# A paged decode step: who asks for the value pages, SyncE one by one or GpSimd with indirect transfers

## The reference

```
kv_past = cache_kv[page_table, l]            # 8 sequences x 16 pages of 128 rows
q, k, v, logf, gates = project_in(h, ...)    # 16 heads: 4 stick-breaking, 6 dilated, 6 forgetting
o_sb  = stick_breaking_attention(q_sb, k_sb_all, v_sb_all, q_pos, k_pos)
o_fox = forgetting_attention(q_fox, k_fox_all, v_fox_all, cum[:, p:], cum, q_pos, k_pos)
o_dil = merge_dilation_groups(...)           # three window buffers per sequence
x = x + gate1 * (merged @ w_o);  x = x + gate2 * hier_moe(...)
```

## Time and profile before

| | |
|---|---|
| median of 3 runs | 1397.74 us (1393.3 to 1398.04) |
| the profiled execution, its own time | 1395.3 us |
| its span, first to last instruction | 1393.6 us |
| PE busy | 1175.0 us (84%) |
| DVE busy | 436.0 us (31%) |
| ACT busy | 293.7 us (21%) |
| POOL busy | 232.2 us (17%) |
| moved by DMA | 306.60 MB, mean 220 GB/s |
| mean granted clock | 0.921 |

### The profile page before, as it was taken

How to read it: one execution, slowest core, us unless ns; L and a number is a source line. 1 busy time by engine, 2 the same in 40 slices (tenths; PEclk the granted TensorE clock), 3 DMA queues, 4 the chain that set the end, 5 groups by cost and what they waited for, 6 DMA issues and landing times.

```text
span 1393.6 us, 21222 instructions
## 1 busy us (share of the span) xinstructions
PE 1175.0 (84%) x7743; PEld 794.1 (57%) x7743; DVE 436.0 (31%) x1072; ACT 293.7 (21%) x629; POOL 232.2 (17%) x321
## 2 busy tenths in 40 slices
PE   5699999987899999986788788878999479989890
PEld 3477777555577777764555555656735345445440
DVE  4200000264332223313344344442634601111116
ACT  2211010143222222222232232222211011111112
POOL 1000000050011112220000000000000046556530
PEclk9899999998889999999998899997999579899895
DMA  8743333139445421049988889995721479999965
GB/s 298 278 176 128 123 122 110 31 121 301 142 192 183 154 92 47 17 148 317 298 290 262 289 287 301 303 334 201 272 95 46 166 293 381 352 410 402 413 227 197
DMA packets 112838, 306.60 MB, mean 220 GB/s; under 512 B 18966, under 2 KB 33071, under 8 KB 103472
## 3 DMA queue, kind: packets, MB, share of 16 engines
q1 hardware_dynamic: 95600, 251.93, 50.8%
q0 software_dynamic: 16576, 49.10, 9.4%
q10 hardware_dynamic: 576, 4.46, 0.9%
HBM read 304.35 MB, written 45.81 MB: 251 GB/s over the span
## 4 chain that ended last, share of the span: by engine, by line
PE 62%; SPq 15%; issue 8%; DVE 8%; DMA 5%; ACT 2%; POOL 0%; POOLq 0%; DVEq 0%; ACTq 0%
PE psum L940 56%; SPq L608 6%; SPq L612 6%; DVE arena L1846 2%; PE psum L1512 1%; SPq L550 1%; PE psum L1250 1%; DMA wring<-in_w_mod 1%; PE psum L1168 1%; DMA arena<-in_cache_kv 1%; DMA xT<-in_cache_kv 1%; DVE wring L1854 1%; PE psum L1537 1%; DVE wring L1846 1%; DMA hT<-gate_tiles 1%
## 5 line engine op out<-in xcount | busy, mean ns | idle before, releaser
L940 PE MATMUL psum<-hT,wring 128*128 128x272 f32 x1216 | 292.6, 399 | 11.4 <-ACT hT L1568 11.4
L940 PEld LDWEIGHTS psum<-hT,wring 128*128 128x128 f32 x1216 | 230.6, 192 | 76.6 <-issue 15.1
L940 PE MATMUL psum<-arena 128*8 128x128 f32 (+6 forms) x1540 | 179.4, 350 | 12.7 <-issue 7.6
L940 PEld LDWEIGHTS psum<-arena 128*8 128x8 f32 (+4 forms) x1540 | 90.6, 113 | 76.5 <-issue 60.4
L940 PE MATMUL psum<-wring,arena 128*8 128x128 f32 (+3 forms) x976 | 108.0, 390 | 7.2 <-DVE wring L1846 3.5
L940 PE MATMUL psum<-hT,arena 128*128 128x272 f32 (+1 forms) x300 | 77.5, 447 | 19.2 <-issue 10.1
L842 POOL TENSOR_SCALAR wring<-wring,arena 128x384 f32<-128x384 f32 (+6 forms) x32 | 45.7, 1427 | 254.5 <-DVE arena L2102 254.5
L1250 PE MATMUL psum<-small,arena 128*128 128x128 f32 x392 | 63.8, 319 | 27.7 <-DMA arena<-in_cache_kv 24.6
L940 PEld LDWEIGHTS psum<-wring,arena 128*8 128x8 f32 (+3 forms) x976 | 49.7, 109 | 58.3 <-issue 52.4
L790 ACT COPY arena<-psum 128x512 f32<-128x512 f32 x80 | 46.6, 585 | 166.6 <-PE psum L1250 113.0
L1250 PEld LDWEIGHTS psum<-small,arena 128*128 128x128 f32 x392 | 52.7, 165 | 38.2 <-issue 34.1
(11 more groups left out here) (243 smaller groups left out, 1361.7 us busy)
## 6 DMA issues: line engine op xcount, KB each, us to landing
arena<-in_cache_kv SPq DMA_DIRECT2D x128, 320.0 KB, 3.5
wring<-in_w_mod SPq DMA_DIRECT2D x10, 2048.0 KB
xT<-in_cache_kv SPq DMA_DIRECT2D x64, 320.0 KB, 3.6
wring<-in_cache_kv SPq DMA_DIRECT2D x64, 320.0 KB, 3.6
wring<-in_w SPq DMA_DIRECT2D x20, 1024.0 KB
out_dil_sample<-in_cache_dil SPq DMA_DIRECT2D x8, 2044.0 KB, 11.0
arena<-in_w SPq DMA_DIRECT2D x27, 512.0 KB
wring<-in_w_in SPq DMA_DIRECT2D x6, 2048.0 KB
```

The source lines that it names most:

```text
L940: return T.matmul(out, lhsT, rhs, start=start, stop=stop, **k)
```

## The change

SP no longer asks for value pages. The page numbers of all 128 pages are loaded once to all partitions (`v_ids`) and DVE computes from them a table of row numbers, `v_at` = 256 * page + 2 * partition + 1, kept in the storage of `rstd`. POOL asks for each value page with one indirect DMA that takes its 128 row numbers from a column of the table. POOL's loop is unrolled: it asks for all 16 pages of sequence 0 first; then, for each b, it waits for `seq_pv` b, loads `vncur`, asks for the first eight pages of sequence b+1, waits for `sp_ready`, does the four additions, and asks for the other eight. SP's wait for `v_used` is gone; ahead of page 9 it waits for `seq_pv`, since the window rows still share a buffer. DVE waits for the page numbers ahead of the stick-breaking scores.

```diff
+            sp.dma_start(v_ids, I["page_table"].rearrange("(o b) n -> o (b n)", o=1).to_broadcast([P, P])
+                         ).then_inc(sem("ld_pt"), 16)
...
-                    if p == half and b0 >= 2:
-
-                        sp.wait_ge(sem("v_used"), i * 2 * PV_STEPS + PV_STEPS * (b0 - 1))
+                    if p == half + 1 and b0 >= 2:
+
+                        sp.wait_ge(sem("seq_pv"), i * 2 + (b0 - 1))
                     if b0 == 0 and p == 4:
                         attention_done()
-                    page(b0, p, 0, kpage[p % 8], f"ld_k{p % 8 // 2}", free)
-                    if p >= half:
-                        values(b0, p - half)
-                    elif b0:
-                        values(b0 - 1, p + half)
+                    page(p, kpage[p % 8], f"ld_k{p % 8 // 2}", free)
                     if p == half + 1:
                         window_rows()
-                if b0 == NB - 1:
-                    for p in range(half, PAGES):
-                        values(b0, p)
...
+            def settle(scrap):
+
+                link(nc.gpsimd.tensor_tensor(scrap, ones[0:1, 0:1], ones[0:1, 0:1], ALU.mult))
+
+            def values(b, lo, hi):
+
+                for p in range(lo, hi):
+                    pool.indirect_dma_start(
+                        out=vpast[b % 2][:, p, :], out_offset=None,
+                        in_=I["cache_kv"].rearrange("n l k a h d -> (n l k a) (h d)"),
+                        in_offset=bass.IndirectOffsetOnAxis(ap=v_at[:, PAGES * b + p:PAGES * b + p + 1], axis=0)
+                        ).then_inc(sem(f"ld_v{b % 2}"), 16)
+
+            for n in range(2):
+                pool.wait_ge(sem(f"st_g{n}"), 16 * 3)
...
+            pool.wait_ge(sem("v_rows"), 1)
+            settle(pool_scrap)
+            values(0, 0, PAGES)
+            for b in range(NB):
+                if b:
+                    pool.wait_ge(sem("seq_pv"), b)
+                pool.dma_start(vncur[0:NT, :], vs_d[b * NT:b * NT + NT, :]).then_inc(sem("ld_vn"), 16)
+                if b + 1 < NB:
+                    settle(pool_scrap)
+                    values(b + 1, 0, PAGES // 2)
+                pool.wait_ge(sem("sp_ready"), b + 1)
+                sp_, w, y = s_sp, s_w[:, b % 2, :], s_y
...
+                nc.gpsimd.tensor_tensor(y[:, 0:256], w[:, 0:256], w[:, 128:384], ALU.add
+                                        ).then_inc(sem("y_ready"), 1)
+                if b + 1 < NB:
+                    values(b + 1, PAGES // 2, PAGES)
...
+            dve.wait_ge(sem("ld_pt"), 48)
+            ts(v_at, v_ids, 256.0, value_row, ALU.mult, ALU.add).then_inc(sem("v_rows"), 1)
```

More of the change, by code:

```diff
@@ L611, in page @@
                         sp.wait_ge(sem("kT_mm"), free)
-                    sp.dma_start(dst, pg[:, :, kv].rearrange("o k h d -> k (o h d)")).then_inc(sem(done), 16)
-                def values(q0, p):
-                    page(q0, p, 1, vpast[q0 % 2][:, p, :], f"ld_v{q0 % 2}")
+                    sp.dma_start(dst, pg[:, :, 0].rearrange("o k h d -> k (o h d)")).then_inc(sem(done), 16)
                 def window_rows():
@@ L849, in _ @@
             link(nc.gpsimd.memset(s_y[:, 256:320], 0.0))
[L850 to L856, removed]
-                    sp_, w, y = s_sp, s_w[:, par, :], s_y
-                    link(nc.gpsimd.tensor_tensor(w[:, 0:256], sp_[:, 0:256], sp_[:, 16:272], ALU.add))
-                    link(nc.gpsimd.tensor_tensor(y[:, 0:256], w[:, 0:256], w[:, 32:288], ALU.add))
-                    link(nc.gpsimd.tensor_tensor(w[:, 0:256], y[:, 0:256], y[:, 64:320], ALU.add))
-                    nc.gpsimd.tensor_tensor(y[:, 0:256], w[:, 0:256], w[:, 128:384], ALU.add
-                                            ).then_inc(sem("y_ready"), 1)
-                link.leave(NB // 2)
+            def settle(scrap):
+                link(nc.gpsimd.tensor_tensor(scrap, ones[0:1, 0:1], ones[0:1, 0:1], ALU.mult))
@@ new lines, in _ @@
+            pool.wait_ge(sem("o_ev"), 8)
+            pool.wait_ge(sem("w_used"), 12)
+            pool.wait_ge(*done_at("new_ready"))
+            for stored in ("st_k", "st_v"):
+                pool.wait_ge(sem(stored), 16 * KV_STORES)
+            pool.wait_ge(sem("st_smp"), 16 * SAMPLE_STORES)
+            pool.wait_ge(sem("st_lf"), 32)
+            pool.wait_ge(sem("v_rows"), 1)
[10 more added lines that the diff above has]
+                sp_, w, y = s_sp, s_w[:, b % 2, :], s_y
+                link(nc.gpsimd.tensor_tensor(w[:, 0:256], sp_[:, 0:256], sp_[:, 16:272], ALU.add))
+                link(nc.gpsimd.tensor_tensor(y[:, 0:256], w[:, 0:256], w[:, 32:288], ALU.add))
+                link(nc.gpsimd.tensor_tensor(w[:, 0:256], y[:, 0:256], y[:, 64:320], ALU.add))
+                nc.gpsimd.tensor_tensor(y[:, 0:256], w[:, 0:256], w[:, 128:384], ALU.add
+                                        ).then_inc(sem("y_ready"), 1)
+                if b + 1 < NB:
+                    values(b + 1, PAGES // 2, PAGES)
@@ L868, in _ @@
             pool.wait_ge(*done_at("slots_ready"))
-            def settle():
-                link(nc.gpsimd.tensor_tensor(carried[0:1, :], ones[0:1, 0:1], ones[0:1, 0:1], ALU.mult))
             def gather(m):
@@ L877, in gather @@
                     pool.wait_ge(sem("xg_t"), 2 * (m - RING) + 2)
-                    settle()
+                    settle(carried[0:1, :])
                 pool.indirect_dma_start(
@@ L1339, in weigh_values @@
                 if hi < PAGES:
-                    last.then_inc(sem("v_used"), 1)
                     return
```

12 lines of the change are left out of this document (8 added, 4 removed).

## The result

| | before | after |
|---|---|---|
| median | 1395.52 us (4 runs) | 1470.39 us (1465.21 to 1473.95, 4 runs) |
| ratio, 95% interval | | 1.0519 (1.048 to 1.0558) |
| the profiled execution, its own time | 1395.3 us | 1471.75 us |
| its span; mean granted clock | 1393.6 us; 0.921 | 1469.7 us; 0.896 |
| loads of `vncur`, second to eighth | 694.21 to 934.96, 40.1 us each | 709.96 to 1008.20, 49.7 us each |

A forecast was written before the change was run, and what follows sets the result against it. SP's issuing (36.7 us per sequence), PE and the DMA engines were taken to lie close together as bounds. -18.8 (six sequences) - 2 (start) + 0.4 (front) = -20.4 us gave 1377 us, range 1364 to 1402 us.

The forecast's parts named there:

- Six sequences: 6 x (40.1 - 37.0) = 18.8 us less: Decode stage: each of six sequences would shorten from 40.1 to 37.0 us, 18.8 us less in all.
- pitch of 37.0 us: Decode time per sequence: PE's own 36.5 us plus 0.5 us, with an indirect DMA taken as 1.30 us.
- A page lands 3.6 us after its issue ... PE should find its keys there: Decode key pages: SP asks eight pages ahead, over 14 us of PE's work, so PE should not wait for keys.
- DMA engines, 34.4 us per sequence: Decode: 11.7 MB per sequence at 339 GB/s take 34.4 us, only 6% below PE's 36.5 us.
- The rival that made them the bound: Decode: mixed pages reach at most 300 GB/s, 38.9 us per sequence, 1396 us in all, no change; chance 0.17.
- POOL: Decode: indirect DMAs 1.26 us apart, 26 of 36.5 us per sequence, no bound; PE waits 0 to 0.3 us for additions.
- Late additions: Decode rival: eight indirect DMAs at up to 1.77 us delay POOL's additions, PE waits about 3.4 us, 1412 us; chance 0.23.
- PE's own pace, 36.5 us: Decode: PE's time per sequence without waits for pages, the middle of 35.9 and 37.2 us from two sequences.
- The start, 2 us less: First two decode sequences: 2 us less taken, between bounds of 14 us less and 6 us more.
- even sharing: First two decode sequences: POOL's and SP's queues share DMA evenly, so the first sequence ends 6 us later.
- Front, +0.4 us: Before decode: SP's extra page-number load ahead of the 80 small stores costs one issue, 0.4 us more.
- the waits of SP and DVE that I costed at nothing: SP's `seq_pv` wait ahead of page 9 is free; DVE's 2.1 us wait for page numbers hides under PE's 8.75 us.

The follow-up runs named there:

- e12: The changed kernel itself run again, unaltered, on chip 5: 1406.22 us, ratio 1.0064 to the kernel before.
- e18: The changed kernel with only 32 of 128 rows of each value page fetched, on chip 15: 1374.40 us, ratio 0.9846 to the kernel before.
- e11: The changed kernel in its own order, indirect transfers spaced 1.80 us apart, on chip 9: 1402.31 us, ratio 1.0038 to the kernel before.
- e10: The changed kernel with four pages before the additions and twelve behind, transfers 1.47 us apart, on chip 9: 1381.49 us, ratio 0.9887 to the kernel before.
- e5: The changed kernel with plain transfers on POOL's queue and a fifth of each value row, on chip 0: 1372.01 us, ratio 0.9811 to the kernel before.
- e8: The changed kernel with only 32 of 128 rows of each value page fetched, on chip 0: 1371.85 us, ratio 0.9822 to the kernel before.
- e17: The changed kernel with four pages before the additions and twelve behind, transfers 1.47 us apart, on chip 15: 1381.21 us, ratio 0.9901 to the kernel before.
- e9: The changed kernel with four pages before the additions and twelve behind, unspaced, on chip 9: 1386.52 us, ratio 0.9898 to the kernel before.
- e13: The changed kernel with four pages before the additions and twelve behind, unspaced, on chip 5: 1389.89 us, ratio 0.9946 to the kernel before.
- e16: The changed kernel with four pages before the additions and twelve behind, unspaced, on chip 15: 1387.26 us, ratio 0.9963 to the kernel before.
- e15: The changed kernel in its own order, indirect transfers spaced 1.80 us apart, on chip 13: 1407.69 us, ratio 1.0075 to the kernel before.
- e4: The changed kernel with plain transfers on POOL's queue, page number read into a register, on chip 13: 1416.67 us, ratio 1.0143 to the kernel before.
- e1: The changed kernel with value pages asked for two at a time as PE turns key pages, on chip 13: 1411.28 us, ratio 1.0105 to the kernel before.
- e3: The changed kernel fetching 128 of 640 floats of each value row, same bursts, on chip 13: 1471.32 us, ratio 1.053 to the kernel before.

## Why the prediction was wrong, step by step

**"Six sequences: 6 x (40.1 - 37.0) = 18.8 us less"** is the step that failed. Behind its pitch of 37.0 us stand two things that were wrong; this is the first. It put a price on indirect transfers by the time they take POOL, and gave other engines none. On chip 13 they cost (1.0508 - 1.0064), 4.4% or 62 us, in PE's waits for events: the larger part of the loss. No row shown before hinted at it and no rival named it. The trace of the kernel before did carry the chip's mark in its MoE (28 missing records of 288), but PE lost nothing by it there: from 1200 to 1210 us it is busy 10.00 of 10.00 us.

**"A page lands 3.6 us after its issue ... PE should find its keys there"** is the second. That latency was measured with keys and values on one queue, in the order of need; with two full queues it was 9 to 10 us (e12). On chips without the hold-up the forecast was -1.5% (20.4 us) and e12 measured +0.64%, a gap of 29 or 30 us. With a quarter of the rows in each value page, the order alike, e18 stands at -1.5%, 2.2% or 30 us below e12. That this is the forecast's own number is in part luck: e18's pitch of 37.9 us is 0.9 above the forecast's, 5 us in six sequences, and its first two sequences end 6 us earlier than before, at 688.13 us, where 2 were forecast.

**DMA engines, 34.4 us per sequence**: mis-sized. They run at 396 GB/s when both queues are full, so 11.7 MB take 29.5 us, and in e12's sequences they then stand idle for a quarter of the time (share 0.71 to 0.79 where it was 0.92). Bandwidth was less short than I thought, and its order in time mattered more. The rival that made them the bound, 1396 us, is close to e12 by number only.

**POOL**: right. 1.26 us each, and in e12 the additions start 11.05 us after `seq_pv` and end at 14.2; PE waits for them only 2.5 us in the whole stage. The port-pair rule of the Trainium skill that I weighed ("SBUF — State Buffer", the box on the "DVE blocks DMA" trap) doesn't show here: 64 indirect DMAs of the page buffers take 952 to 1077 ns, median 957, with DVE busy a third of each sequence. The rule holds for DVE operations in a two-port mode, and whether any of those beside the transfers ran in one, no run here tells.

**Late additions**, the rival for the slower side: right sign, wrong mechanism. But its price for such a wait was good. e11 fulfils its condition (1.80 us each, 1.77 in the rival), and PE then does wait, for POOL's last addition. The list of PE's waits in e11:

```profile
PE psum L961 <- POOL arena L885: 8.1, 5, 2.0
```

Its pitch is 40.8 us where the rival's sum gave 41.4; e11 is 1.5% above e10.

**PE's own pace, 36.5 us**: 37.7 to 37.9 in e5, e8, e10, e17 and e18, 1.2 us too low for each sequence, 7 us in all. I had taken the middle of two sequences of the kernel before and no loss of clock.

**The start, 2 us less**: measured 15.8 us more (709.96 against 694.21), of it the 15.04 us wait shown above. On chip 5 it was 2.8 us more (697.05), within my bounds of 14 less to 6 more, and near the even sharing that I chose.

**Front, +0.4 us, and the waits of SP and DVE that I costed at nothing**: right, by the rows above.

So with its order mended the idea does what was forecast, nearly: e10 and e17, four pages ahead and twelve behind, 1.47 us apart, are 1.1% and 1.0% faster than the kernel before, and the fastest that leave nothing out. The same order unspaced gave 1.0%, 0.5% and 0.4% (e9, e13, e16). Chip 13 has seen neither.

## What to carry to other kernels

Two queues that are both full don't share by need: what is asked for early on one delays what is needed next on the other, by the bytes of their packets. Where a latency was measured with one queue, bound it again with the second one full before you rely on it. A queue of close indirect transfers may cost engines that have nothing to do with it; space them (e15, 1.0075 on the chip that suffers), or use plain transfers with a page number in a register where a page is contiguous (e4 there: no hold-up, but 1.0143, since bursts of plain transfers delay the keys too). Look in the trace of the old kernel for idle time without a releaser near its own indirect transfers: it marked the chip here. And run the changed kernel itself again beside each experiment: in e5 to e8 I took for the work of my edits what was also a change of chip.

## What was unexpected of the hardware

On one of five numbered chips (13), 128-row indirect DMAs issued 1.26 us apart delay semaphore updates of PE and single instructions of SP's sequencer: a 29 ns MOVE takes up to 707 ns, an event comes up to 14 us late. There the delay outlives the burst a little. Eight transfers started at 710.98 us end on POOL at 720.9, and PE's next transposes start at 723.24:

```profile
723.24 2.39 PE L1269 MATMUL psum<-small,xT 128*128 128x128 f32 x10 [6.30 <-DVE xT L2246]
```

In the records the delay ends at 722.4 us, 11.4 us after the burst began, and at 647.3, 33.9 us after the first of 24: 1.42 us for each transfer, an estimate of what that chip takes to serve one. That fits the 1.80 us of e15, which left no copy idle for an event (though a MOVE of 469 ns), and the pairs of e1, which held 31 us and not 91. It doesn't go with fewer bytes (e3) and isn't seen with plain transfers on the same queue (e4). The same chip's traces also lack 25 to 37 of 288 update records in the MoE, those of four others none. What in the chip does it, and what sets this chip apart, these runs don't tell. The kernel before takes the same time on every chip used, 1395 to 1398 us at the median.
